# Residual carried by the scattered expert rows, and a new order of the ranked experts

## What is computed

```python
h = rms_norm(x, g_moe[l]) * (1.0 + scale_m[:, None]) + shift_m[:, None]
# per token: the best of 4 groups, the best 2 of its 8 experts, softmax weights times the group's probability
for e in range(N_EXPERTS):                      # 32
    hid = jax.nn.silu(jnp.dot(h, w_gate[e])) * jnp.dot(h, w_up[e])
    y = y + gates[:, e:e + 1] * jnp.dot(hid, w_down[e])
x = x + gate_m[:, None] * y
...
return rms_norm(x, g_final)
```

## Time and profile before

| | us |
|---|---|
| runs shown | 1008.69, 1006.54, 1008.46 (median 1008.46) |
| the profiled execution, its own time | 1007.81 |
| its span, first to last instruction | 1006.0 |
| mean granted TensorE clock | 0.987 of full speed |
| PE busy | 953.2 (95% of the span) |
| DVE, ACT, POOL busy | 594.4, 400.9, 119.5 |
| DMA | 189.88 MB, mean 189 GB/s over the span |

### The profile page before, as it was taken

How to read it: one execution, slowest core, us unless ns; L and a number is a source line. 1 busy time by engine, 2 the same in 40 slices (tenths; PEclk the granted TensorE clock), 3 DMA queues, 4 the chain that set the end, 5 groups by cost and what they waited for, 6 DMA issues and landing times.

```text
span 1006.0 us, 15057 instructions
## 1 busy us (share of the span) xinstructions
PE 953.2 (95%) x5352; PEld 520.0 (52%) x5352; DVE 594.4 (59%) x1597; ACT 400.9 (40%) x909; POOL 119.5 (12%) x219
## 2 busy tenths in 40 slices
PE   3899999999999999999999999999899999998984
PEld 2465576444447856677766555556533433333421
DVE  3388647999999799987777333456422222232217
ACT  6131135666660388877668221212211111121113
POOL 3001000000007510110000000000111111111004
PEclk9899999999999999999999999998999999998999
DMA  9997100110102000040000411089799999999979
GB/s 325 334 358 277 43 22 21 43 41 22 42 23 47 1 1 1 2 169 22 1 2 2 167 45 40 23 352 382 307 409 422 421 419 421 420 420 421 418 296 367
DMA packets 70381, 189.88 MB, mean 189 GB/s; under 512 B 10200, under 2 KB 37136, under 8 KB 58016
## 3 DMA queue, kind: packets, MB, share of 16 engines
q1 hardware_dynamic: 62176, 170.53, 44.2%
q0 software_dynamic: 5760, 16.78, 4.3%
q10 hardware_dynamic: 2368, 1.57, 0.6%
HBM read 174.17 MB, written 18.89 MB: 192 GB/s over the span
## 4 chain that ended last, share of the span: by engine, by line
PE 65%; DVE 20%; DMA 6%; issue 4%; SPq 2%; ACT 1%; POOL 1%; POOLq 0%; DVEq 0%; ACTq 0%
PE PS L2031 12%; PE PS L1908 11%; DVE BIAS L1168 8%; PE PS L2054 6%; PE PS L1801 6%; PE PS L1844 5%; PE PS L1866 4%; DMA X<-in_w_down_dram 3%; PE PS L1762 3%; PE PS L1714 3%; PE PS L1861 2%; DVE X L1232 2%; PE PS L1739 2%; PE PS L1679 2%; PE PS L2018 2%
## 5 line engine op out<-in xcount | busy, mean ns | idle before, releaser
L1714 PE MATMUL PS<-HT,X 128*128 128x512 f32 x384 | 168.8, 593 | 0.0
L1714 PEld LDWEIGHTS PS<-HT,X 128*128 128x128 f32 x384 | 72.5, 190 | 92.4 <-issue 92.4
L878 ACT ACTIVATE X<-X,nmx 128x128 f32<-128x128 f32 (+7 forms) x128 | 98.4, 770 | 51.5 <-DVE nmx L1232 51.0
L2031 PE MATMUL PS<-QKV,HT 128*32 128x512 f32 (+2 forms) x560 | 113.0, 594 | 2.4 <-ACT HT L976 1.7
L1908 PE MATMUL PS<-QKV,HT 128*128 128x512 f32 x256 | 113.7, 597 | 0.0
L1168 DVE TENSOR_SCALAR_CACHE_REDUCE BIAS<-SC,W 128x384 f32<-128x384 f32 (+3 forms) x128 | 96.4, 809 | 1.1
L1526 DVE TENSOR_TENSOR HT<-PS,HT 128x256 f32<-128x256 f32 x20 | 8.5, 425 | 140.9 <-ACT HT L984 140.9
L861 ACT ACTIVATE X<-SC,W 128x896 f32<-128x896 f32 x64 | 69.6, 1088 | 43.0 <-DVE W L1156 43.0
L1801 PE MATMUL PS<-QKV 64*128 64x512 f32 (+3 forms) x384 | 79.0, 517 | 1.6 <-DVE nmx L1232 1.1
L1908 PEld LDWEIGHTS PS<-QKV,HT 128*128 128x128 f32 x256 | 47.4, 190 | 53.7 <-issue 53.6
L1844 PE MATMUL PS<-ident,X 128*128 128x128 f32 x432 | 63.2, 279 | 2.1 <-DVE X L1250 2.0
(11 more groups left out here) (306 smaller groups left out, 1544.9 us busy)
## 6 DMA issues: line engine op xcount, KB each, us to landing
QKV<-in_w_down_dram SPq DMA_DIRECT2D x20, 1024.0 KB, 24.5
QKV<-in_w_gate_dram SPq DMA_DIRECT2D x19, 1024.0 KB, 17.3
QKV<-in_w_up_dram SPq DMA_DIRECT2D x19, 1024.0 KB, 20.4
QKV<-in_w_ada_dram SPq DMA_DIRECT2D x8, 2048.0 KB, 12.5
QKV<-in_w_ada_dram SPq DMA_DIRECT2D x8, 1024.0 KB, 12.4
X<-in_w_in_dram SPq DMA_DIRECT2D x16, 512.0 KB, 3.8
X<-in_w_down_dram SPq DMA_DIRECT2D x8, 1024.0 KB, 22.3
QKV<-expert_rows SPq DMA_DIRECT2D x16, 512.0 KB, 10.3
```

The source lines that it names most:

```text
L878: act.activation(sc, sc, ACT.Exp, bias=nmx[:, i % 4, m:m + 1], scale=-1.0, accum_out=rs[:, i, m:m + 1]).then_inc(exp_done, 1)
L1714: end = pe.matmul(PS[:, 2 * b + half, :], WS[:, b, j, :], HT[:, j, BANK * half:BANK * (half + 1)], start=(j == 0), stop=(j == KC - 1))
L2031: end = pe.matmul(PS[at, 2 + b, :], hgT[b][:, P * c_ + at.start:P * c_ + at.stop], WGU[w][:, c_, :, :], start=(c_ == 0), stop=(c_ == KC - 1))
```

## The change

It has two parts.

**The rows carry the residual and the weights.** Gathered rows and results now share four buffers, `held`. `ev_y` is two DVE instructions for each half: the product of the PSUM result, a weight per row and `out_row`, written back to PSUM, and then `held` times `is_first` plus that PSUM result, written over the gathered rows. So a token's first expert's row holds residual plus weighted result, and the second's row only the weighted result; the sum of both is what the last norm needs. The buffer is in use from its gather to the landing of its scatter, so `gather(n+3)` now waits for `scatter(n-1)`, the last user of the same buffer.

```diff
             def gather(n):
-                if n >= 2:
+                if n >= 4:
+                    pool.wait_ge(y_out[n % 2], 16 * (n // 2 - 1))
+                elif n >= 2:
                     pool.wait_ge(t_ps, n - 1)
-                pool.indirect_dma_start(out=xg[n % 2], out_offset=None, in_=h2_dram,
+                pool.indirect_dma_start(out=held[n % 4], out_offset=None, in_=h2_dram,
...
             for n in range(NSTEP):
-                if n + 4 < NSTEP:
-                    gather(n + 4)
+                if n >= 1 and n + 3 < NSTEP:
+                    gather(n + 3)
                 scatter(n)
...
-            def ev_y(e, b, stored):
-                dve.wait_ge(y_out[b], stored * 16)
+            def ev_y(e, buf, weight, is_first, counted):
                 for h in range(2):
                     part = slice(BANK * h, BANK * (h + 1))
                     dve.wait_ge(dn_ps, 2 * e + h + 1)
-                    dve.tensor_tensor(ysb[b][:, part], PS[:, 5 + h, :], out_row[:, part], ALU.mult).then_inc(y_sb, 1)
+                    dve.scalar_tensor_tensor(out=PS[:, 5 + h, :], in0=PS[:, 5 + h, :], scalar=weight, in1=out_row[:, part],
+                                             op0=ALU.mult, op1=ALU.mult).then_inc(hh_done, 1)
+                    dve.wait_ge(hh_done, counted + h + 1)
+                    dve.scalar_tensor_tensor(out=held[buf][:, part], in0=held[buf][:, part], scalar=is_first,
+                                             in1=PS[:, 5 + h, :], op0=ALU.mult, op1=ALU.add).then_inc(y_sb, 1)
```

```diff
             dve.wait_ge(modc_set, 1)
+            weigh_experts()
+            link(dve.tensor_scalar(row_first[:, 0:NSTEP], PS[:, 2, NSTEP:2 * NSTEP], float(S) + 0.5, None, ALU.is_lt))
+            spread_weights(low_tok, NSTEP, weight_is)
             ev_t(0, 0)
-            weigh_experts()
-            dve.wait_ge(out_row_in, 32)
-            ev_hid(0, 0)
+            dve.wait_ge(sel_ps, 5)
+            link(keep_weights(0, PS[:, 6, 0:3 * NSTEP], NSTEP))
+            ev_hid(0, 0, 0)
```

Gone are `x2_back`, the diagonal matrices, PE's sums of `XT`, and one of the two instructions of `combine`:

```diff
-                    back = {last_use[25]: range(0, 6), last_use[26]: range(6, T)}
-                    if n - 1 in back:
-                        for t in back[n - 1]:
-                            sp.dma_start(XT[:, t, :], h2_dram[P * t:P * (t + 1), :]).then_inc(x2_back, 16)
...
-                link(dve.scalar_tensor_tensor(out=XT[:, t, :], in0=y1, scalar=w1[:, t:t + 1], in1=XT[:, t, :],
-                                              op0=ALU.mult, op1=ALU.add))
-                dve.scalar_tensor_tensor(out=XT[:, t, :], in0=y2, scalar=w2[:, t:t + 1], in1=XT[:, t, :],
-                                         op0=ALU.mult, op1=ALU.add).then_inc(cb_done, 1)
+                dve.tensor_tensor(XT[:, t, :], y1, y2, ALU.add).then_inc(cb_done, 1)
```

**Another order.** `SEQ` changes:

```diff
-    SEQ = [25, 26, 5, 23, 3, 12, 31, 14, 29, 20, 0, 7, 9, 16, 17, 6, 27, 4, 28, 19, 21, 8, 13, 11, 18, 30, 1, 10, 2, 24, 22, 15]
+    SEQ = [10, 22, 30, 15, 24, 7, 0, 31, 18, 27, 9, 21, 29, 16, 12, 20, 19, 6, 14, 11, 5, 28, 17, 23, 3, 1, 2, 8, 25, 26, 13, 4]
```

More of the change, by code:

```diff
@@ L755, in _ @@
                 pool.wait_ge(ov_list, 2)
+                for b in range(2):
+                    pool.wait_ge(y_out[b], 16 * uses(b))
                 with pool.Fori(0, NOV // 2) as i:
@@ L1011, in _ @@
             act.dma_start(gfin, g_final.partition_broadcast(P)).then_inc(act_in, 16)
-            for i, t in enumerate(mixed):
-                for k in range(2):
-                    act.activation(diag[:, i, k, :], ident[:, :], ACT.Copy, scale=rt[:, 5 + k, t:t + 1]
-                                   ).then_inc(diag_done, 1)
             for t in range(T):
@@ L1492, in weigh_experts, with spread_weights, keep_weights @@
                 link(dve.tensor_scalar(eps_row[:, 0:T], eps_row[:, 0:T], EPS, None, ALU.mult))
+                both = rt[:, 5:7, :]
+                link(dve.tensor_copy(weight_part[0], both))
+                link(dve.tensor_tensor(weight_rest, both, weight_part[0], ALU.subtract))
+                link(dve.tensor_copy(weight_part[1], weight_rest))
+                link(dve.tensor_tensor(weight_part[2], weight_rest, weight_part[1], ALU.subtract))
+            def spread_weights(low, tiles, out_):
+                for a in range(3):
+                    end = dve.scalar_tensor_tensor(out=out_[:, :, :, a, :], in0=low, scalar=0.0,
+                                                   in1=weight_part[a].unsqueeze(3).to_broadcast([P, 2, T, tiles]),
+                                                   op0=ALU.is_gt, op1=ALU.mult)
+                    end.then_inc(weights_at, 1)
+            def keep_weights(first, ps, tiles):
+                return dve.tensor_reduce(row_weight[:, first:first + tiles], ps.rearrange("p (a n) -> p n a", a=3), AX_X,
+                                         ALU.add)
             def place_overflow():
@@ L2061, in weights_of, with list_weights @@
                         sorted({(w % places, 16 * (w // places + 1)) for w, _, _ in parts[n]}))
-            turn_rows(0, 0, 16)
+            def list_weights(bank, at, tiles, rows, weights):
+                for q in range(T):
+                    for k in range(2):
+                        end = pe.matmul(PS[:, bank, at:at + 3 * tiles], rows[:, k, q, :],
+                                        weights[:, k, q, :, :].rearrange("p a n -> p (a n)"),
+                                        start=(q == 0 and k == 0), stop=(q == T - 1 and k == 1))
+                return end
+            turn_rows(0, 0, 16, 0)
+            pe.wait_ge(weights_at, 3)
+            list_weights(6, 0, NSTEP, row_is, weight_is).then_inc(sel_ps, 1)
             gate_up(0, 0, *weights_of(0, GUS))
-            turn_rows(1, 1, 16)
+            turn_rows(1, 1, 16, 1)
             for n in range(NSTEP):
```

76 lines of the change are left out of this document (44 added, 32 removed).

## The result

The changed kernel takes **1021.96 us** (median of 4 runs, 1020.21 to 1024.32); the kernel before took 1008.23 beside it (1006.54 to 1008.69). The ratio is 1.0141, with an interval of 1.0116 to 1.0165: 14 us slower. Forecast were 1012.4 in a range of 1003.5 to 1019. The direction was right, the size was not: +4.6 us were forecast and +14.7 came in the profiled execution.

A forecast was written before the change was run, and what follows sets the result against it. PE's chain bounds the expert stage, with DMA weight loads close behind; gathers waiting for scatters become the new pace. 5.5 (stage) + 0.75 (DVE) - 1.7 (end) = +4.6 us on 1007.81, so 1012.4 us, range 1003.5 to 1019.

The forecast's parts named there:

- the order of the experts: Expert stage: the new order changes nothing on the chain while gathers pace the steps.
- the start costs nothing: Before step 0: the added DVE instructions fit DVE's idle time ahead of `ev_t(0)`; 0, up to +1 us.
- `x2_back` is worth nothing: Eight 512 KB transfers go, about 10 us of DMA time; worth 0 on the chain.
- the signs that the prediction gave: Expert stage: 16 waits for gathers, 10 to 12 us in all; steps of 12.7 us; no late weights; clock up.
- G: Way from the end of `down_proj(n-1)` to the start of `turn_rows(n+3)`: 20.7 us, against 19.53 at PE's own pace.
- link: Two steps of the even or odd chain: G plus `turn_rows` and `down_proj`, 25.36 us instead of 24.2, eight per chain.
- it takes 8 to 8.7 us, and I take 8.6: The scatter's term in G: time from a scatter's issue to its landing, 8.6 us.
- rival 3: Expert stage: scatter and gather hold each other up, G above 21.3, 1020 us at 21.7; chance 0.14.
- The clock should stay up in the stage: Expected sign: PE's clock does not fall during the expert stage.
- each 0.1 us of G is 0.8 us: Expert stage: a change of 0.1 us in G moves the kernel's time by 0.8 us.
- -1.7: End: DVE adds a tile in one instruction, -1.7 us; bounds 2.6, or nothing if expert-row loads set the end.
- Rival 2: Expert stage: G below 20.0, rows in time, weights the bound; 1003.5 us, up to 1006; chance 0.27.

The follow-up runs named there:

- e1: The changed kernel with the old order of the experts put back: 1019.78 us, ratio 1.0110 to the kernel before.
- e2: The kernel before with only the new order of the experts: 1007.06 us, ratio 0.9999.
- e5: The kernel before with only the wait added, gather(n+3) behind the landing of scatter(n-1): 1018.25 us, ratio 1.0115 to the kernel before.
- e3: The changed kernel with a fifth buffer for rows, so that gather(n+4) waits for scatter(n-1): 1004.90 us, ratio 0.9975 to the kernel before.
- e10: The changed kernel with two useless matmuls on PE ahead of each wait for gathered rows from step 4 on: 1021.22 us, ratio 1.0135 to the kernel before.
- e9: The changed kernel with a third DVE instruction for each half in `ev_y`: 1026.04 us, ratio 1.0196 to the kernel before.
- e6: The changed kernel with one DVE instruction for each half in `ev_y` instead of two, residual left out: 1017.87 us, ratio 1.0114 to the kernel before.
- e12: The changed kernel with five buffers, the old order of the experts, and scatter(n) issued ahead of gather(n+4): 1003.82 us, ratio 0.9974 to the kernel before.
- e4: The changed kernel with five buffers and the old order of the experts: 1011.22 us, ratio 1.0036 to the kernel before.
- e8: The changed kernel loading only the first quarter of each expert weight matrix in the steps: 998.41 us, ratio 0.9923 to the kernel before.

## Why the prediction was right and wrong

**The mechanism was right.** Gathers wait for scatters and PE for gathers, no weight is late, the order of the experts changes nothing that can be told (e1 and e2), and the start costs nothing. e5 and e3 show the wait as the cause from both sides. That `x2_back` is worth nothing was not tested by itself. Of the signs that the prediction gave, PE waited 17.1 us in eleven waits in place of 10 to 12 us in sixteen, and a step took 13.4 us in place of 12.7.

**The size of G was wrong, and so was the count of what a link holds.** The forecast had 25.36 us for each of eight links, 202.9. The even chain took 213.9 (739.18 to 953.11), in seven links in which PE waits for rows and one, in the pause of the weight loads, at PE's pace. These 11.0 us more, 0.8 more at the end and 1.7 less ahead of step 0 make up the difference between the forecast +4.6 and the +14.7 of the profiled execution. From the pieces of the even chain:

| seven links | forecast | measured |
|---|---|---|
| `down_proj` to issue of the scatter | 16.1 | 17.0 |
| scatter (8.6 each) | 60.2 | 65.3 |
| landing to issue of the gather | 5.5 | 5.7 |
| gather (8.7 each) | 60.9 | 63.5 |
| landing to `turn_rows`, and 0.2 for late landings | 2.3 | 0.3 |
| `turn_rows` and `down_proj` | 32.6 | 38.8 |
| sum | 177.6 | 190.6 |
| the eighth link | 25.4 | 23.4 |

**The step that failed is "it takes 8 to 8.7 us, and I take 8.6", the scatter's term in G.** On the even chain the scatters took 9.3 us each, 5.1 us more in all, and slow matmuls added 5.8. The odd chain, of the same length, shows the term more clearly: its seven scatters outside the pause took 71.2 us, 10.2 each and 11.0 more than forecast, while its `turn_rows` and `down_proj` took the 32.6 of the forecast (in two links the rows lay ready for 1.6 and 2.1 us while PE ran slow matmuls). In e5, where the clock was up from 740 us on, the scatters of 10.1 us were there as well, and the loss too. The 8.6 was read from a scatter issued 4.35 us behind a gather, and the change moves the two together. The prediction saw this under rival 3, "the next scatter is issued while the gather is still in flight", and met it with "that is so today as well". It is so, but the distance counts. For the first link's scatter (10.6, which is 2.0 of the 5.1 us) the cause is open, and the kernel before has it too. The gathers were low by 0.4 each. Rival 3, with 1020 us, was the nearest of the cases, and its chance of 0.14 was too low.

**The clock was missed.** "The clock should stay up in the stage" did not hold: it falls three times, where PE waits for several us, and on this chain slow matmuls are 5.8 of the 6.2 us in the row of `turn_rows` and `down_proj`. The price is not additive, though. e10 has the clock up and no time back that can be told, and e5 loses 11.6 us with the clock up. So it is a part of this trace's chain, larger even than the scatter's 5.1, but the loss does not need it.

**DVE.** The instructions take 0.77 and 0.76 us instead of 0.69, and the last result comes 0.8 later as forecast. The rule "each 0.1 us of G is 0.8 us" fits e9 (0.73 us for each link, 5.5 us in all by the ratios), and is too high for e6 (3 us in place of 6.4 and 0.8); with some 4 us of uncertainty in each, the scatters' medians of 9.1 and 10.1 us say more for the queue taking a part back than these times do.

**The end.** -1.7 was forecast for the end without DVE's 0.75, and 0.9 came. POOL's root is indeed no longer held up: all eight take 0.54 to 0.57 us, where the slowest took 1.60 us and more before. But that is not what ends the program now. The prediction's reason for a gain of nothing weighs more: expert rows land until 1007.7 us, and DVE waits for PE's sum. One profiled execution doesn't tell this from the low clock that the end has in both kernels.

**Rival 2 describes the kernel with one buffer more.** Its price, 1003.5 to 1006 with rows in time and weights late, is where e3 (1004.9) and e12 (1003.8) came out. It needed a fifth buffer, not a smaller G.

What stays open: why the new order is 6 us better than the old in e3 and e4. That the pause near 785 us, in which indirect transfers take 3.8 us, lets POOL catch up fits the traces of e3, e4 and e12, but is only argued; no run took it away alone.

## What to carry to other kernels

When a load is made to wait for a store of the same queue, add up the whole way from the last reader to the first user, and take the duration of each transfer with what will stand ahead of it in the queue, not with what stands there today. If that sum comes near the time that the buffers give (here 20.7 us by forecast and 21.7 measured, against 19.5), take one more buffer: it was worth 17 us. Issuing what is ready ahead of what has to wait was worth 6 us with one order of the experts and cost 3 to 4 with the other, where weights then came late, so ask what becomes the bound next. Before you count an engine's saved microsecond on such a loop, look whether the transfers get longer by it.

## What the runs showed of the hardware

- An indirect transfer of up to 128 rows of 4 KB (0.42 MB on average, 16.78 MB in 40 transfers) mostly takes 8 to 12 us beside weight loads at 420 GB/s, 3.4 to 4.1 us when these pause in the changed kernel, and 4.0 to 4.3 us (medians) when only a quarter of the weights is loaded (e8).
- Beside weight loads, a scatter issued 1.3 to 3 us behind a gather lands 3.1 to 3.7 us after it in the changed kernel, and 3.3 to 3.8 on average in each of the others that have such pairs.
- PE's granted clock fell to 1.2 GHz in the stage after PE had stood idle for 2.0 to 4.1 us, but not each time: of twelve idle times between 2.0 and 3.0 us in the kernels without useless matmuls, six went with a fall. In e5 it also fell once, at 719.2 us, behind an idle time of 1.65 us. With two or four useless matmuls ahead of every wait it stayed at 1.00 through the stage, in e10 even with one idle time of 3.0 us.
